# Low halves of the weights on VectorE instead of GpSimd in the first block's feed-forward part of a hybrid trunk layer

## What is computed

```python
mix = jnp.concatenate([a, hm], axis=-1) @ w_out
x = x + rmsnorm(mix, g_mix_post)
up = rmsnorm(x, g_ffn_pre) @ w_up                      # 1024 -> 2 x 2816
up, ffn_buf_new = causal_dwconv(up, ffn_buf, w_conv_ffn, b_conv_ffn)   # width 3
f = jax.nn.gelu(up[..., :D_FF], approximate=True) * up[..., D_FF:]
x = x + rmsnorm(f @ w_down, g_ffn_post)
x = x + (p @ w_ple) * jax.nn.sigmoid(rmsnorm(x, g_ple) @ w_ple_gate)
```

## Time and profile before

| | |
|---|---|
| median of 3 runs | 3106.73 us (3101.3 to 3118.31) |
| profiled execution | 3106.95 us, span 3105.1 us |
| granted TensorE clock, mean | 0.943 |
| busy: TensorE, VectorE, ScalarE, GpSimd | 90%, 55%, 29%, 10% of the span |
| chain that ended last, shares | TensorE 73%, VectorE 14%, ScalarE 5%, DMA 3%, GpSimd 2% |
| GpSimd subtracts, line 487 | 108, 311.4 us in all, mean 2889 ns |
| ScalarE high parts, line 789 | 108, 113.8 us in all, mean 1055 ns |

### The profile page before, as it was taken

One profiled execution on the slowest core, in us unless ns is written; L12 is line 12 of the kernel. 1 busy time (PEld: TensorE's weight loads), 2 busy tenths in 40 slices (PEclk: granted clock), 3 DMA queues, 4 the chain that ended last, 5 costly groups with the idle time before them and its releaser, 6 DMA issues.

```text
span 3105.1 us, 39736 instructions
## 1 busy us (share of the span) xinstructions
PE 2799.7 (90%) x14657; PEld 2677.6 (86%) x14657; DVE 1721.3 (55%) x3612; ACT 902.7 (29%) x1862; POOL 311.6 (10%) x112
## 2 busy tenths in 40 slices
PE   6688979888989999998999999889999997699976
PEld 6678878887889999887999998889999886699975
DVE  6955896965355756425556653455856434441532
ACT  3344433333333112423321233332112322221221
POOL 4421455432000000000000000000000000000000
PEclk9889999998989999998999999999999988899987
DMA  8645878866446666553666665456666552366645
GB/s 278 224 149 220 293 255 307 314 246 234 168 163 223 232 234 232 184 218 118 218 235 231 232 229 208 146 180 230 231 232 230 188 200 82 138 240 230 231 176 133
DMA packets 109062, 660.77 MB, mean 213 GB/s; under 512 B 20148, under 2 KB 20408, under 8 KB 39104
## 3 DMA queue, kind: packets, MB, share of 16 engines
q1 hardware_dynamic: 99424, 627.05, 56.7%
q10 hardware_dynamic: 9440, 31.07, 2.7%
HBM read 532.96 MB, written 125.11 MB: 212 GB/s over the span
## 4 chain that ended last, share of the span: by engine, by line
PE 73%; DVE 14%; ACT 5%; DMA 3%; issue 2%; POOL 2%; SPq 0%; ACTq 0%; POOLq 0%; DVEq 0%
PE proj L509 23%; PE proj L510 22%; PE proj L511 22%; DVE cv L1305 3%; DVE mix_room L1566 2%; POOL w_split L487 2%; DVE f_split L1593 2%; DMA w_raw<-in_w_units 1%; DVE mix_room L1563 1%; ACT w_split L789 1%; DVE temp_room L1224 1%; DVE temp_room L1397 1%; DVE mix_room L1212 1%; PE m L542 1%; PE m L627 1%
## 5 line engine op out<-in xcount | busy, mean ns | idle before, releaser
L509 PE MATMUL proj<-h_split,w_split 128*128 128x416 f32 x2720 | 984.0, 362 | 39.5 <-ACT temp_room L1046 12.4
L510 PE MATMUL proj<-h_split,w_split 128*128 128x416 f32 x2720 | 964.2, 354 | 2.5 <-issue 2.5
L511 PE MATMUL proj<-h_split,w_split 128*128 128x416 f32 x2720 | 957.4, 352 | 0.0
L509 PE MATMUL proj<-f_split,w_split 128*128 128x416 f32 x1600 | 592.2, 370 | 72.1 <-ACT mix_room L1109 24.0
L510 PE MATMUL proj<-f_split,w_split 128*128 128x416 f32 x1600 | 576.9, 361 | 0.0
L511 PE MATMUL proj<-f_split,w_split 128*128 128x416 f32 x1600 | 572.9, 358 | 0.0
L509 PEld LDWEIGHTS proj<-h_split,w_split 128*128 128x128 f32 x2720 | 519.8, 191 | 57.1 <-issue 34.8
L511 PEld LDWEIGHTS proj<-h_split,w_split 128*128 128x128 f32 x2720 | 519.4, 191 | 10.8
L510 PEld LDWEIGHTS proj<-h_split,w_split 128*128 128x128 f32 x2720 | 520.0, 191 | 6.1 <-issue 3.2
L509 PEld LDWEIGHTS proj<-f_split,w_split 128*128 128x128 f32 x1600 | 312.4, 195 | 94.2 <-ACT mix_room L1109 28.7
L1305 DVE SCALAR_TENSOR_TENSOR cv<-a_ext,vecs,cv 128x416 f32<-128x416 f32 (+1 forms) x600 | 387.4, 698 | 0.0
(11 more groups left out here) (197 smaller groups left out, 2050.3 us busy)
## 6 DMA issues: line engine op xcount, KB each, us to landing
w_split<-w_kept SPq DMA_DIRECT2D x432, 1024.0 KB, 4.8
w_kept<-w_split SPq DMA_DIRECT2D x108, 1024.0 KB, 7.4
w_raw<-in_w_units SPq DMA_DIRECT2D x108, 512.0 KB, 5.3
x_resid<-in_x ACTq DMA_DIRECT2D x5, 1664.0 KB, 9.7
out_y<-x_resid ACTq DMA_DIRECT2D x10, 832.0 KB, 9.2
rows<-in_x ACTq DMA_DIRECT2D x4, 832.0 KB, 6.4
qkv<-in_x ACTq DMA_DIRECT2D x4, 832.0 KB, 4.7
qkv<-in_p ACTq DMA_DIRECT2D x5, 416.0 KB, 5.2
```

Of the source, the lines that this page charges most:

```text
L509: mm(dst, w_hi, a_hi, start=first, stop=False)
L510: mm(dst, w_hi, a_lo, start=False, stop=False)
L511: return mm(dst, w_lo, a_hi, start=False, stop=last)
```

## The change

The subtracts for the r-th split units of a range, from the fourth unit of up A to the last that is split in down B (63 of 108), are taken from GpSimd's program and put in VectorE's. GpSimd keeps the other 45. In VectorE's program each stands at a place in its hand-written order: for the first group of a pair between `low_f(j - 1)` and `conv_ffn(j)`, for the second behind `conv_ffn(j)` and before the conv taps, and in the down stages one place before each chunk of conv taps or each addition. The loops of GpSimd's program are written out.

```diff
+SPLIT_ON_VECTOR = range(SPLIT_NTH[AT[False].g_upa + RING], SPLIT_NTH[AT[False].u_next - 1] + 1)
...
-            runs = [0] + [r for r in range(1, SPLITS) if split_at(r) != split_at(r - 1) + 1] + [SPLITS]
-            for r0, r1 in zip(runs, runs[1:]):
-                whole = (r1 - r0) // (RAW * RING) * (RAW * RING)
-                if whole:
-                    with pool.Fori(0, whole, RAW * RING) as n:
-                        for r in range(RAW * RING):
-                            low_part(n + (r0 + r), r0 + r)
-                for r in range(r0 + whole, r1):
+            for r in range(SPLITS):
+                if r not in SPLIT_ON_VECTOR:
                     low_part(r, r)
...
+                def low_part(u):
+                    if not opening or u not in SPLIT_NTH or SPLIT_NTH[u] not in SPLIT_ON_VECTOR:
+                        return
+                    r, slot = SPLIT_NTH[u], u % RING
+                    dve.wait_ge(s_hi.sem, r + 1)
+                    v.tensor_tensor(w[:, slot, 1, :], w_raw[:, r % RAW, :], w[:, slot, 0, :].bitcast(F32),
+                                    ALU.subtract).then_inc(s_w[slot].sem, 16)
+
+                def low_parts(g):
+                    for u in USED_UP[False][g]:
+                        if u not in (at.u_dna, at.u_dnb):
+                            low_part(u + RING)
...
                         if j > first:
                             gated(j - 1)
                             low_f(j - 1)
+                        g = (at.g_upb if half else at.g_upa) + 2 * (j - first)
+                        low_parts(g)
                         conv_ffn(j)
+                        low_parts(g + 1)
                         conv_next(half, range(j - first + 10 * half, j - first + 10 * half + 1))
                     gated(first + FH - 1)
                     low_f(first + FH - 1)
+                    low_part((at.u_dnb if half else at.u_dna) + RING)
                     if half == 0:
-                        conv_next(0, range(FH, CW))
-                        conv_next(1, range(10))
+                        for i in range(KD):
+                            low_parts(at.g_dna + i)
+                            if i < 5:
+                                conv_next(0, range(FH + 4 * i, FH + 4 * i + 4))
+                            else:
+                                conv_next(1, range((10 * (i - 5)) // 3, (10 * (i - 4)) // 3))
                 for i in range(KD):
                     dve.wait_ge(s_evac.sem, s_evac.done(blk, at.g_dnb + i + 1))
+                    low_parts(at.g_dnb + i)
                     v.tensor_tensor(out[:, i, :], out[:, i, :], hf[:, i % 4, :], ALU.add).then_inc(s_dnadd.sem, 1)
```

## The result

The changed kernel takes 3152.27 us (median of 4 runs, 3145.31 to 3168.79), the kernel before, run on the same chip, 3112.52 (4 runs, 3101.3 to 3120.6). The ratio is 1.0138, 95% interval 1.0084 to 1.0192: slower by 1.4%. 3132 was forecast, with 3152 as the upper end, which the result passes by 0.3 us. The profiled execution took 3153.57 us with a span of 3151.8, granted clock 0.936; the spans differ by 46.7.

A forecast was written before the change was run, and what follows sets the result against it. In block 0's up stages a closed ring of 7.55 + D was to set the period. Seven stretches (+23.5, -1.4, -15.0, +1.3, +24.5, -2.4, -5.3) sum to +25.2 us on 3106.95, so 3132, range 3100 to 3152.

The forecast's parts named there:

- The ring: Block 0's up stages: closed chain through VectorE's, SyncE's and ScalarE's orders, once per pair; period 7.55 + D, 12.85 us.
- D: Landing time of the raw load in the up stages' ring, taken as 5.3 us, range 4.6 to 6.1.
- the signs listed before: Trace marks in block 0 that would show the forecast right, such as low_f recurring every 12 to 13.6 us.
- the two stretches: Nine periods each of up A and up B in block 0: 91.2 us before, 115.7 after; +23.5 and +24.5.
- The three rows: Raw loads issued 3.5, 4.5 and 4.7 us behind their forerunner, landing in 4.6, 5.2 and 6.1 us.
- step 7: Down B to the first group behind it: 43.4 as in block 1 plus 6.4 late, 49.8 against 55.1, -5.3 us.
- step 3: Down A from its first evacuation to up B: 47.3 against 62.3, with 4.5 of lateness, -15.0 us.
- The start of the ring: Beginning of up A's nine periods: 0.9 us earlier, as GpSimd's 2.4 no longer stands before the first load.
- Steps 2 and 6: From the end of up A's and up B's nine periods to the first down evacuation: -1.4 and -2.4 us.
- A: Rival: ring not closed, VectorE's 8.4 us hides under TensorE's 9.07, up stages at block 1's pace; 3062 us, chance 0.14.
- B: Rival: raw loads land like isolated ones, 4.2 to 4.6 us, down stages at block 1's pace; 3101 to 3119, chance 0.18.
- C: Rival: TensorE's half clock lasts in the up stages, a pair then costs 16 us; 3153 us, chance 0.08.

The follow-up runs named there:

- e4: Changed kernel with raw loads of 256 KB in place of 512 KB in block 0's feed-forward part: 3095.5 us, 0.9978 of the kernel before.
- e5: Changed kernel, only the first subtract of each up pair moved, in front of gated(j-1): 3096.4 us, 0.9979 of the kernel before.
- e8: Changed kernel with three raw slots in place of two: 3090.36 us, 0.9965 of the kernel before.
- e1: Changed kernel, both subtracts of each up pair ahead of conv_ffn(j), before gated(j-1) and before low_f(j-1): 3058.2 us, 0.9864 of the kernel before.
- e2: Changed kernel, the second subtract of each up pair back on GpSimd: 3152.33 us, 1.0165 of the kernel before.
- e9: Changed kernel, SyncE asks for a moved unit's 1 MB store before the raw load instead of behind it: 3176.3 us, 1.0236 of the kernel before.
- e7: Changed kernel, VectorE subtracts in the down stages alone, GpSimd in the up stages: 3091.14 us, 0.9968 of the kernel before.
- e6: Changed kernel, only the second subtract of each up pair moved, between gated(j-1) and low_f(j-1): 3142.78 us, 1.0122 of the kernel before.
- e3: Changed kernel, the first subtract of each up pair back on GpSimd: 3122.96 us, 1.0083 of the kernel before.

## Why the prediction was off in size

**The direction and the mechanism held.** The ring is there with every piece in the chain of waits, and four runs moved its period as its terms say: e4 through D, e5 through which load closes it, e8 through taking the load out, e1 through taking conv out. Most of the signs listed before hold. The low half of f took 0.59; the loads go out 4.3 and 9.2 apart in turn (4.4 and 8.5 forecast); the subtract is 1.22; TensorE waits once per pair for a low half of weights, 2.6 us on average in up A and 3.0 in up B (2 to 4 forecast, 4.2 at most); down A's 17 us wait is gone. Two came out otherwise. The low half of f recurs every 13.0 to 14.2, and 4 of the 18 periods are above the 13.6 that was given. ScalarE waits for the raw unit in front of both high parts of a pair, and its longer wait is the one in front of the first, 5.5 us against 3.2. The forecast saw one ring only: the second one, through SyncE's order, showed itself in e2, and is why e2 missed its expectation by 75 us.

**The step that failed is D.** "I take their mean, 5.3": of after's period, 13.56 and 13.44, 7.55 is the rest of the ring as forecast (6.01, 0.03 and 1.51 against 6.0, 0.02 and 1.5), so D was 6.0 and 5.9. Over the two stretches that is 122.06 + 120.92 less 2 x 115.7, 11.6 of the 16.7 us missing. The three rows were too few, and picked by hand: the trace of before holds 30 raw loads that went out 3.5 to 5.2 us behind their forerunner, and their median is 5.7. With that the sum is 18 x 0.4 = 7 higher, 3139. So D was within its stated 4.6 to 6.1, but the sum took a value too low.

**The reason given for D is shown in part.** The forecast said that such loads are long because the store before is under way. e9's first loads show that a store ahead does lengthen a landing, 5.7 against 4.25. But in e4 a store goes out 3.9 us ahead of the second load as well and is still under way (it lands 5.3 us on, in the median), and the halved second load takes no longer than the first (both 3.2 to 3.3). How much of D = 5.9 is the store and how much the load before stays open.

**Down B, step 7, -5.3 against -2.0.** 6.4 us of lateness were put down; against block 1's 43.4 it is 9.7. TensorE waits there 3.9 for VectorE's subtracts, as forecast in kind, and 3.6 for the first kept unit, which lands 9.54 after a SyncE that is held up by the last subtracts. The forecast followed VectorE's order to its end and not SyncE's. The remaining 2 us go with a granted clock of 0.93: behind the wait for the kept unit, from 717.3 to 722.9, TensorE's matmuls start 0.35 us apart in place of 0.19.

**Small ones.** Down A, step 3: 44.86 against 47.3; that is 2.1 over block 1's 42.8, where 4.5 were put down, and TensorE waits for VectorE's subtracts only 0.9. The start of the ring gained nothing (0.9 forecast). Steps 2 and 6 gave 2.8 less than they should; in step 2 TensorE waits 2.6 for a subtract of VectorE's (at 465.78).

**The rivals.** A, that it ends faster because VectorE's load fits: its premise is true and its end false. The load does fit (e1, e2), but the ring is closed. Its 3062 is what e1 reached, 3058.2, once the subtracts stood elsewhere. The Trainium skill, GPSIMD Engine Reference, section Engine selection, is borne out on the price, 1.22 us on VectorE against 2.34 on GpSimd (e2). By the time, that choice of engine lost 1.4% in the order of the change, gained 0.3% where only the down stages follow it (e7), and gained 1.4% with e1's order. B, landings as isolated ones: no, 5.9; but e5 made them so, 4.3, and came to 3096.4, under the kernel before. C, the half clock lasts: the granted clock was 0.88 and 0.90 in the up stages, and the chain of the pair shows no TensorE, so the clock was not what set the period. TensorE's matmuls do start 0.35 apart for some 3.5 us behind each of its waits (from 398.5 to 402.2), but TensorE is done and waits again before the pair ends. That the time of 3152 came to C's figure is chance.

## What to carry to other kernels

When work moves to an engine whose order is written out by hand, don't add up the engine's load: follow the resource that the work releases (here the raw slot), through every in-order program behind it, until you are back where you began; the length of that ring is the period, and half a microsecond in it counts once per pass. Put the instruction that releases a buffer ahead of the long work it does not depend on, and look at the queue that asks for the next load as one more engine with an order of its own. For a landing in such a ring take the median of all loads of its kind and spacing, not a few.

## What the runs showed of the hardware

- The landing of a 512 KB raw load, each followed by a 1 MB store, medians in the up stages: 4.25 us where the load before had gone out 8 us or more earlier (after, e5), 5.9 at 4.3 us behind it (after, 5.4 to 6.7), 5.9 at 2.3 us as well (e5, 5.5 to 7.6), and 7.1 at 0.9 us (e2, e6, 7.0 to 8.5). A store placed directly ahead added 1.5 to the first of these and 0.3 to the second (e9). In e1, where the DMA engines are 96% busy from 340 to 420 us, the median there was 5.9 all the same.
- With half the bytes, 256 KB, both loads of a pair landed in 3.2 to 3.3 us, where 512 KB took 4.25 and 5.9 (e4). What halving saved differs: 1.0 us on a load with an idle queue, 2.7 on one behind other traffic.
- GpSimd's subtract and some of VectorE's instructions hold each other up. VectorE's 128x416 subtract takes 0.59 alone and 2.46 to 2.53 beside GpSimd's, its 128x4 copy 0.16 and 2.35 (e3). GpSimd's takes 2.34 while VectorE stands still or is itself held, and 17.12 beside conv taps that run on without a pause.
